# Router fed from raw rows, and weight splits moved into the value tiles, in a two-layer retention/attention trunk with a routed mixture of experts

## The reference, cut to what matters

```python
h = h + mix
hn = rmsnorm(h, ffn_norm[layer]).reshape(B * S, D)      # x * rsqrt(mean(x*x) + EPS) * g
h = h + hier_moe(hn, ...)

# in hier_moe: 4 groups of 8 experts, top-1 group, top-2 experts in it
grp_logits = (xt @ w_grp) + b_grp
exp_logits = (xt @ w_exp) + b_exp
hid = silu(xk @ w_gate[e]) * (xk @ w_up[e])
y = hid @ w_down[e]                                     # weighted by the gates, added per token
```

## Time and profile before

| | us |
|---|---|
| median of 3 runs (lowest, highest) | 1517.93 (1515.38, 1518.26) |
| the profiled execution | 1517.55 |
| its span, first to last instruction | 1515.7 |

### The profile page before, as it was taken

One profiled execution on the slowest core, in us unless ns is written; L12 is line 12 of the kernel. 1 busy time (PEld: TensorE's weight loads), 2 busy tenths in 40 slices (PEclk: granted clock), 3 DMA queues, 4 the chain that ended last, 5 costly groups with the idle time before them and its releaser, 6 DMA issues.

```text
span 1515.7 us, 16138 instructions
## 1 busy us (share of the span) xinstructions
PE 1186.6 (78%) x6928; PEld 712.2 (47%) x6928; DVE 434.6 (29%) x834; ACT 340.7 (22%) x560; POOL 64.8 (4%) x119
## 2 busy tenths in 40 slices
PE   4999996858667667576999899996857677577575
PEld 4986785413323133132788767776413133133131
DVE  4754535100100101003766534635100101001001
ACT  3334422101001001012655444642101001001010
POOL 2000000000000000000300051030000000000000
PEclk8999997988878898797999989996988789688888
DMA  8552476999999999998545554457999999999996
GB/s 307 180 195 103 193 277 234 420 421 421 421 421 422 421 421 421 422 421 349 146 167 184 203 110 123 172 168 312 373 421 421 421 421 421 422 421 422 421 421 264
DMA packets 90778, 489.02 MB, mean 323 GB/s; under 512 B 6385, under 2 KB 6449, under 8 KB 41041
## 3 DMA queue, kind: packets, MB, share of 16 engines
q1 hardware_dynamic: 86736, 480.55, 78.7%
q0 software_dynamic: 3968, 7.42, 2.8%
HBM read 486.77 MB, written 1.17 MB: 322 GB/s over the span
## 4 chain that ended last, share of the span: by engine, by line
PE 58%; DMA 34%; DVE 4%; issue 1%; SPq 1%; ACT 1%; POOL 0%; ACTq 0%; DVEq 0%
DMA ring<-in_exp_down 20%; DMA ring_more<-in_exp_down 13%; PE bank L1004 8%; PE triple L1043 7%; PE triple L344 7%; PE triple L345 7%; PE triple L346 7%; PE bank L1079 4%; PE triple L1060 4%; PE bank L1060 2%; PE bank L344 2%; PE bank L346 2%; PE bank L345 2%; DMA ring<-in_ret_w_in 1%; PE bank L1426 1%
## 5 line engine op out<-in xcount | busy, mean ns | idle before, releaser
L1043 PE MATMUL triple<-ring,work 128*32 128x512 f32 x1344 | 251.4, 725 | 84.9 <-DMA ring<-in_exp_up 53.5
L1043 PE MATMUL triple<-ring_more,work 128*32 128x512 f32 x704 | 161.0, 720 | 38.8 <-DMA ring<-in_exp_up 25.6
L1043 PEld LDWEIGHTS triple<-ring,work 128*32 128x32 f32 x1344 | 63.9, 129 | 218.4 <-issue 218.4
L1153 DVE TENSOR_TENSOR work<-work,triple 128x512 f32<-128x512 f32 x16 | 11.0, 688 | 529.3 <-PE triple L1043 529.3
L1060 PE MATMUL triple<-ring,work 128*32 128x512 f32 x344 | 93.8, 910 | 78.5 <-DMA ring<-in_exp_down 41.6
L1004 PE MATMUL bank<-work,hn 128*128 128x128 f32 x512 | 125.8, 407 | 16.5 <-DVE h L1162 12.2
L1004 PEld LDWEIGHTS bank<-work,hn 128*128 128x128 f32 x512 | 123.2, 335 | 27.9 <-issue 23.4
L1162 DVE TENSOR_TENSOR h<-h,bank 128x512 f32<-128x512 f32 x64 | 44.0, 687 | 279.7 <-PE bank L1079 279.7
L326 DVE TENSOR_TENSOR lo_b<-ring,hi_b 128x2048 fp32r<-128x2048 f32 x40 | 90.0, 2288 | 21.3 <-ACT hi_b L319 21.3
L1043 PEld LDWEIGHTS triple<-ring_more,work 128*32 128x32 f32 x704 | 39.2, 128 | 102.9 <-issue 102.9
L1060 PE MATMUL triple<-ring_more,work 128*32 128x512 f32 x168 | 60.2, 922 | 33.4 <-DMA ring<-in_exp_down 29.5
(11 more groups left out here) (280 smaller groups left out, 1791.3 us busy)
## 6 DMA issues: line engine op xcount, KB each, us to landing
ring<-in_exp_down SPq DMA_DIRECT2D x43, 2048.0 KB, 32.6
ring<-in_exp_gate SPq DMA_DIRECT2D x42, 2048.0 KB, 32.9
ring<-in_exp_up SPq DMA_DIRECT2D x42, 2048.0 KB, 33.0
ring_more<-in_exp_gate SPq DMA_DIRECT2D x22, 2048.0 KB, 32.9
ring_more<-in_exp_up SPq DMA_DIRECT2D x22, 2048.0 KB, 33.5
ring_more<-in_exp_down SPq DMA_DIRECT2D x21, 2048.0 KB, 32.5
ring<-in_ret_w_in SPq DMA_DIRECT2D x12, 2048.0 KB, 9.3
ring<-in_w_kv SPq DMA_DIRECT2D x12, 2048.0 KB, 8.8
```

The source lines that it names most:

```text
L1043: last = nc.tensor.matmul(bank[2 + kind][rows, :], m_x[:, k, rows], w[e][:, kk * FF:(kk + 1) * FF], start=(k == 0), stop=(k == KD - 1))
```

## The change

**Router, both layers.** `norm_act` and `norm_dve` with i = 1, 3 are replaced by `ffn_norm_act` and `ffn_norm_dve`. PE transposes the raw rows `h`, eight pieces of t = 0 as soon as both of its halves have been added, then eight of t = 1 (`raw_transpose_pe`); three PSUM banks are copied whole (128x512) by ACT, one by DVE. The gain goes into `w_route` beforehand (`gained_routes`, one DVE product of 128x288 ahead of L646). PE makes all logits of t = 0, then those of t = 1. The norm's factor is multiplied onto the logits, in the operation that adds the bias, one for each t. `hn` = h * factor is now made by ACT, after the root, and the gather of the first group waits for it. The table for the root is loaded ahead of the wait for `h`.

**Value stage.** The split that stood whole after v2, v3 and v4 is now cut into its halves, one in each of the six units: v4 in m_ = 0, 1, v5 in m_ = 2, 3, the next tile in m_ = 4, 5. ACT does its half first in the unit, DVE between inverted and biased(m_, 1). The number of splits is the same, and what follows v5 stands where it stood.

PE has as many matmuls as before, of the same shapes; none is added. The changes of waits on counters follow from these two.

```diff
+        def ffn_norm_act(act, i):
+            nc.scalar.activation(root_of_no_use[0:1, i:i + 1], ident[0:1, 0:1], ACT.Sqrt)
+            act.wait_ge(s_h, H_DONE[i] - 2)
+            nc.scalar.activation(hn[:, 0, :], h[:, 0, :], ACT.Square, accum_out=stat[:, 0, 0:1]).then_inc(s_sq, 1)
+            for b in range(3):
+                act.wait_ge(s_tp, 4 * i + b + 1)
+                nc.scalar.copy(raw_T(b), raw_bank(b)).then_inc(s_xT_act, 1)
+            act.wait_ge(s_var, i + 1)
+            nc.scalar.activation(stat[:, 2, 0:TT], stat[:, 1, 0:TT], ACT.Sqrt).then_inc(s_std, 1)
+            act.wait_ge(s_rstd, i // 2 + 1)
+            for t in range(TT):
+                nc.scalar.mul(hn[:, t, :], h[:, t, :], stat[:, 1, t:t + 1]).then_inc(s_hn, 1)
+
+        def ffn_norm_dve(dve, i):
+            dve.wait_ge(s_h, H_DONE[i])
...
+            dve.wait_ge(s_tp, 4 * i + 4)
+            nc.vector.tensor_copy(raw_T(3), raw_bank(3)).then_inc(s_xT_dve, 1)
...
+        def raw_transpose_pe(pe, i):
+            for b in range(4):
+                if b % 2 == 0:
+                    pe.wait_ge(s_h, H_DONE[i] - 2 + b)
+                for k in range(4):
+                    last = nc.tensor.transpose(bank[RAW_BANKS[b]][:, k * P:(k + 1) * P],
+                                               h[:, b // 2, 4 * (b % 2) + k::KD], ident)
+                last.then_inc(s_tp, 1)
...
         def route_pe(pe, layer):
...
+            pe.wait_ge(s_wg, layer + 1)
+            for t in range(TT):
+                for k in range(KD):
+                    if k % 4 == 0:
+                        b = 2 * t + k // 4
...
+                    last = nc.tensor.matmul(bank[2 + t][:, 0:36], xT[:, k, t * P:(t + 1) * P],
+                                            w_route[:, k, :], start=(k == 0), stop=(k == KD - 1))
+                last.then_inc(s["logits"], 1)
...
             for m_ in range(6):
                 v, t = 3 + m_ // 2, m_ % 2
+                split_act(act, FIRST_QKV + v_tile(v) + 1, (t,))
                 if m_ < LATE:
                     exps(m_, 0)
...
                 if 1 <= m_ <= LATE:
                     inverted(m_ - 1)
+                split_dve(dve, FIRST_QKV + v_tile(v) + 1, (t,))
                 if m_ < LATE:
                     biased(m_, 1)
```

More of the change, by code:

```diff
@@ new lines, in gained_routes, with raw_bank, raw_T @@
+        def gained_routes(dve, layer):
+            dve.wait_ge(m[layer]["route_w"], 16 * 4)
+            nc.vector.tensor_tensor(w_route[:, :, :], w_route[:, :, :],
+                                    gains[:, 1 + 2 * layer, :].unsqueeze(2).to_broadcast([P, KD, MG + NE]),
+                                    ALU.mult).then_inc(s_wg, 1)
+        RAW_BANKS = (6, 7, 0, 1)
+        def raw_bank(b):
+            return bank[RAW_BANKS[b]].rearrange("p (k s) -> p k s", k=4)
+        def raw_T(b):
+            return xT[:, 4 * (b % 2):4 * (b % 2) + 4, b // 2 * P:(b // 2 + 1) * P]
@@ L398, in batches_done @@
         def batches_done(i, b, by_act):
-            before = sum((4, 2, 8, 2)[:i])
-            return before + (b + 1 if i in SPLIT_NORMS else b // 2 + 1)
+            before = sum(((4, 3, 8, 3) if by_act else (4, 1, 8, 1))[:i])
+            return before + (b + 1 if by_act or i in SPLIT_NORMS else 1)
         def transpose_pe(pe, i):
@@ L428, in transpose_act @@
         def transpose_act(act, i, out, g, before=0, order=None):
-            split = i in SPLIT_NORMS
-            for b in range(4) if split else (0, 2):
+            for b in range(4):
                 act.wait_ge(s_tp, 4 * i + b + 1)
@@ L435, in transpose_act @@
                     src = tp_bank[b][:, (k % 2) * S:(k % 2 + 1) * S]
-                    dst = (out[0] if split else out)[:, k, :]
+                    dst = out[0][:, k, :]
                     if order:
@@ L442, in transpose_dve @@
         def transpose_dve(dve, i, out, g, before=0, order=None):
-            split = i in SPLIT_NORMS
-            for b in range(4) if split else (1, 3):
+            for b in range(4):
                 dve.wait_ge(s_tp, 4 * i + b + 1)
-                if split:
-                    dve.wait_ge(s_xT_act, batches_done(i, b, True) + before)
+                dve.wait_ge(s_xT_act, batches_done(i, b, True) + before)
                 for k in (2 * b, 2 * b + 1):
                     src = tp_bank[b][:, (k % 2) * S:(k % 2 + 1) * S]
[L450 to L459, removed]
+                    dst, high = out[1][:, k, :], out[0][:, k, :].bitcast(F32)
+                    if order:
+                        src = order(src)
+                        dst, high = (v.rearrange("p (a u) -> p a u", a=CLASSES) for v in (dst, high))
+                    last = nc.vector.scalar_tensor_tensor(
+                        out=dst, in0=src, scalar=gains[:, g, k:k + 1],
+                        in1=high, op0=ALU.mult, op1=ALU.subtract)
                 last.then_inc(s_xT_dve, 1)
         def xT_ready(engine, i):
-            if i not in SPLIT_NORMS:
-                engine.wait_ge(s_xT_act, batches_done(i, 2, True))
             engine.wait_ge(s_xT_dve, batches_done(i, 3, False))
@@ L886, in route_dve @@
             L = tmp(TT, 36)
-            dve.wait_ge(s["logits"], 1)
-            dve.wait_ge(s["route_w"], 16 * 4)
-            chain(V.tensor_tensor(L, triple[:, 0:1024].rearrange("p (t c) -> p t c", t=TT)[:, :, 0:36],
-                                  over_tiles(b_route[:], 36), ALU.add))
+            for t in range(TT):
+                dve.wait_ge(s["logits"], t + 1)
+                last = V.scalar_tensor_tensor(out=L[:, t, :], in0=bank[2 + t][:, 0:36], scalar=stat[:, 1, t:t + 1],
+                                              in1=b_route[:, :], op0=ALU.mult, op1=ALU.add)
+            chain(last)
             def first_max(scores, n):
```

65 lines of the change are left out of this document (34 added, 31 removed).

## The result

| | before | after |
|---|---|---|
| median of 5 runs (lowest, highest), us | 1515.57 (1514.56, 1518.26) | 1488.57 (1487.21, 1489.13) |
| the profiled execution | 1517.55 | 1487.21 |
| ratio of the times, 95% interval | | 0.9815 (0.9801 to 0.9828) |

The ratio makes it 28.0 us faster, between 26.1 and 30.2. The forecast was 1493.3 with a range of 1490 to 1501.

A forecast was written before the change was run, and what follows sets the result against it. It took DMA to bound the expert stretches, with work ahead of each gather paid in full, and PE to bound attention. 12.3 + 4.4 + 7.5 = 24.2 off 1517.55 gave 1493.3 us, range 1490 to 1501.

The forecast's parts named there:

- What bounds the kernel: Expert stretches bound by DMA; the pauses before them make work ahead of the gather paid in full; PE bounds attention.
- Change 1, the value stage: Value stage: halved splits remove two PE stalls and the lower clock behind them, 12.3 us, between 6 and 13.
- walk through m_ = 0: First value-stage unit followed operation by operation: no PE wait with halved splits, 1.9 us margin, 7.8 us long.
- rule weighed: Skill page's ramp penalty under 1% of span, so omitted from models; forecast kept the value stage's 5.1 us clock loss.
- Change 2, the router: Norm and router: shorter path from last addition to bias, 4.4 us in layer 0 and 7.5 in layer 1.
- clock allowance of 0.8: Router matmuls, each layer: 0.8 us deducted from the gain for a clock fall near their end.
- transposes' 2.50: Sixteen raw-row transposes ahead of the router, each layer: 2.50 us at full clock.
- A: Value stage: splits inside the tile make a new stall, half its gain stays away, 1499.3 us; chance 0.12.
- B: Value stage and both routers: waits go but the clock stays low, 15.2 us gained, 1502.3 us; chance 0.07.
- C: Both layers' routers run at 1.2 GHz throughout, value stage as forecast, 2.4 us more each, 1498.1 us; chance 0.14.
- E: Router's gain does not arrive: late first tiles or gather waiting for ACT's hn, about 1505 us; chance 0.03.
- D: Value stage: biased waits behind a half split, a 7.1 us stall in all six units, 1535 us; chance 0.02.

The follow-up runs named there:

- experiment 2: Kernel before, with only the split of v4 cut into halves (m_ = 0, 1), later splits left whole: 1511.40 us, ratio 0.9954.
- Experiment 3: Kernel before, with seven, then four useless 128x512 matmuls while PE waits for the norm in both layers: 1514.11 us, then 1511.54 us.
- experiment 5: Changed kernel with the router's eight t = 1 matmuls made twice in both layers: 1495.52 us; its sixteen stretches come from eight other traces of the new router.
- experiment 4: Changed kernel with DVE's half of the split moved ahead of biased(m_, 0) in the value stage: 1496.61 us, ratio 0.9865.
- router_only: Kernel before with the router's part of the change alone, the value stage's splits left whole: 1501.16 us, ratio 0.9896.

## Why the prediction was right in its places and short in its size

**What bounds the kernel.** Right. The pauses stay, shorter by 5.8 and 9.0 us without any load (4.4 and 7.5 forecast, as the router's terms), the stream stays at 1.01, and every gain ahead of the gather and in the value stage is in the span.

**Change 1, the value stage.** Right: 12.57 against 12.3. m_ = 0 took 7.94 (7.8), m_ = 2 13.29 (13.15), the waits are 0.4. The walk through m_ = 0 held, and splitting the price into waits (7.66) and the clock behind them (5.1) was needed: the gain is the sum. That it came so near is partly luck of the execution: experiment 2 shows the clock's part of the second stall alone vary by 1.3 us. On the rule weighed there: the measured 12.57 is the figure with the clock. By the sentence of the Trainium skill ("TensorE: Matmul & The Clock Gate", Part 1, on what is actually happening) the clock's part could have been left out of a model; the trace shows it as two fifths of this term. The size that the page gives holds here, since the clock's parts of all three terms, 11.5 us, are 0.8% of the span; but for the price of a change the trace decides against leaving it out.

**Change 2, the router.** This is the step that failed: the mechanism is right, two terms of its sum were mis-sized. Forecast 4.4 and 7.5, measured 5.89 and 9.06: 1.5 short in each layer.
- The clock allowance of 0.8 in each layer ("a fall near the end"). It measured nothing in the trace of after: 32 records at 1.00. I took small matmuls for the cause of the low clock in the earlier trace rows. Experiment 3 shows another: with the idle time filled, the same matmuls run at 1.00 in all four stretches traced. So the idle time ahead had made the clock low from their start. That the kind of work has no part isn't shown: in five of the sixteen stretches of experiment 5 the clock falls in these matmuls with no idle time ahead, for 0.05 to 0.5 us. The allowance was right in kind and too large in size, by at least 0.3 us a layer and by all of it in this trace.
- The transposes' 2.50, from the earlier trace rows. They took 1.94 or 1.95 in the chain, as they do in experiment 3 (1.9 to 2.0); half a microsecond in each layer. The row was at full clock as I read it, in before:

```profile
183.77:186.27 2.50, 2.50 (x17) 2.28 (x18) 2.50 (x5) 2.42 (x5) 0.00 (x0) 1.00 1.00 419
```

But there each group of four waits in the code until DVE has emptied a bank, and DVE's subtractions took 0.61 us each (seven in 4.28), four of them 2.45. That this pace made the 2.50 is argued, not tried; the new code has no such wait.
- The rest, 0.1 to 0.2 a layer, is the router's matmuls: 3.51 where I had 3.6.

**Rivals.** A and B fell with the trace (no new wait, clock 1.00 in each unit). C fell with it too: in no trace of the new router is more than about the last microsecond of its matmuls at the lower level. E fell with the stretches of the table, 15.26 us to the gather, which DVE released and not ACT. D's mechanism exists (experiment 4), but its price isn't a full stall in each unit.

**The range.** The time is 4.7 us below the forecast: 3.3 by the three terms (27.5 against 24.2), 2.8 by stretches that the change doesn't touch, less 1.4 by which the median of after lies above its profiled execution. The range failed at its fast end, in two ways. The end of each term was the cost at full clock by the row I had, 13 + 5.2 + 8.3 = 26.5, while the traces gave 27.5. And the sum was made against one execution, 1517.55, where the median of before is 1515.57; from that median the same 24.2 gives 1491.4, inside the range. There was nothing for the stretches that the change doesn't touch. These alone gave 2.8 us between the two traces, and 3.7 the other way between two executions of the same changed kernel (first release to the end in layer 1: 450.65 and 454.31). An end for that of 2 to 3 us would have held the time. The times of before gave the hint: the profiled execution and the median were near the top of 1515.4 to 1518.3, and one of three runs was at the bottom.

## What to carry to other kernels

In these traces a long wait of PE costs its length and then the lower clock behind it. When work is moved so that PE doesn't wait, the matmuls that follow get cheaper too, though nobody edited them; here that was 6.4 of the 15.0 us won at the routers. Price both by a row of the same kind of work at 2.4 GHz, and ask whether that row was paced by something else, as the 2.50 us of transposes may have been. Set the base and the range by several executions and not by one. Where the loads pause for a buffer, ask when the second buffer comes free and not only the first.

## What was not expected of the hardware

- The same stretch of the same code, norm and router, takes 21.2 us in some executions and 23.5 to 24.3 in others: its matmuls of 128x36 run in 3.9 to 4.3 or in 6.88 us, by the clock alone.
- The clock can fall while PE is busy without a gap, in the router's matmuls of 128x36 (router_only, 234.50 to 235.60: 0.53); in other executions of the same code it stays at 1.00 through them.
- Matmuls of no use, put into an idle time, make a kernel faster: four of them in each layer 6.5 us (some 4 to 9) in before.
- The clock can be at 1.00 when PE goes idle and at 0.50 when it resumes 5 us later (after, 1468.25 to 1473.20).
- Between the last matmul and the end of the span it is 3.2 us in some executions and 4.8 to 5.2 in others.
